# Four rounded-weight products, then four remainder products: the order of TensorE's matmuls within a unit of a split-precision decoder trunk

## What is computed

```python
def swiglu(h, w_gate, w_up, w_down):
    return (jax.nn.silu(h @ w_gate) * (h @ w_up)) @ w_down

for l in range(DEPTH):                                   # 2 layers
    x = x + 0.5 * swiglu(rmsnorm(x, norm_ffn1_g[l]), ffn1_w_gate[l], ffn1_w_up[l], ffn1_w_down[l])
    h = rmsnorm(x, norm_mix_g[l])
    proj = h @ w_in[l]                                   # 1024 x 5120
    ...
    merged = jax.nn.sigmoid(g_attn) * (attn @ w_branch_attn[l]) \
        + jax.nn.sigmoid(g_conv) * (conv @ w_branch_conv[l])
    x = x + merged @ w_out[l]
    x = x + 0.5 * swiglu(rmsnorm(x, norm_ffn2_g[l]), ffn2_w_gate[l], ffn2_w_up[l], ffn2_w_down[l])
return rmsnorm(x, final_g)
```

## Time and profile before

| | |
|---|---|
| median of 3 runs | 1111.26 us (1111.18 to 1115.11) |
| the profiled execution's own time | 1111.28 us |
| its span, from first to last instruction | 1109.5 us |
| TensorE matmuls | 6512, busy 1089.9 us (98%) |
| weight loads | 6512, busy 962.4 us (87%) |
| VectorE, ScalarE busy | 829.7 us (75%), 642.5 us (58%) |
| mean granted clock of TensorE | 0.995 of full speed |
| read from HBM | 199.32 MB, 181 GB/s over the span |

### The profile page before, as it was taken

One profiled execution on the slowest core, in us unless ns is written; L12 is line 12 of the kernel. 1 busy time (PEld: TensorE's weight loads), 2 busy tenths in 40 slices (PEclk: granted clock), 3 DMA queues, 4 the chain that ended last, 5 costly groups with the idle time before them and its releaser, 6 DMA issues.

```text
span 1109.5 us, 19933 instructions
## 1 busy us (share of the span) xinstructions
PE 1089.9 (98%) x6512; PEld 962.4 (87%) x6512; DVE 829.7 (75%) x1016; ACT 642.5 (58%) x908; POOL 19.9 (2%) x38
## 2 busy tenths in 40 slices
PE   7999999999999999999999999999999999999996
PEld 6888888888899988888888888888888998888885
DVE  5876767778898877776777776767788988677666
ACT  7655544556775655554465555445667656565454
POOL 6100000000000000000000000000000000000000
PEclk9999999999999999999999999999999999999998
DMA  8756555654566566656556656566455655656551
GB/s 221 243 180 199 175 169 188 208 172 152 175 188 188 170 193 187 190 178 191 191 167 186 206 172 198 162 208 194 147 157 184 195 175 184 202 173 205 173 190 39
DMA packets 202462, 201.76 MB, mean 182 GB/s; under 512 B 7904, under 2 KB 201472, under 8 KB 202416
## 3 DMA queue, kind: packets, MB, share of 16 engines
q1 hardware_dynamic: 200288, 199.25, 58.7%
q0 software_dynamic: 992, 1.87, 0.8%
q10 hardware_dynamic: 1136, 0.05, 0.1%
HBM read 199.32 MB, written 1.84 MB: 181 GB/s over the span
## 4 chain that ended last, share of the span: by engine, by line
PE 97%; ACT 1%; DMA 1%; DVE 1%; issue 0%; SPq 0%; DVEq 0%; ACTq 0%
PE acc L1114 57%; PE acc L1123 31%; PE acc L1118 4%; DMA raw<-in_ffn_w_gate_dram 1%; PE mixed L1118 1%; PE score L1118 1%; PE score L1224 0%; PE mixed L1156 0%; PE mixed L1123 0%; PE score L1123 0%; PE mixed L1245 0%; ACT w_hi L474 0%; PE mixed L1232 0%; PE mixed L1238 0%; ACT L508 0%
## 5 line engine op out<-in xcount | busy, mean ns | idle before, releaser
L1114 PE MATMUL acc<-xm,w_hi 128*128 128x512 f32 x2048 | 648.3, 398 | 4.3 <-ACT xt L565 2.4
L758 DVE TENSOR_TENSOR w_lo<-raw,w_hi 128x1024 fp32r<-128x1024 f32 (+1 forms) x387 | 455.7, 1200 | 141.9 <-ACT w_hi L474 141.2
L1123 PEld LDWEIGHTS acc<-xm,w_lo 128*128 128x128 f32 x2048 | 386.0, 188 | 91.5
L474 ACT CAST w_hi<-raw 128x1024 fp32r<-128x1024 f32 (+1 forms) x387 | 389.4, 1030 | 124.9 <-PE acc L1123 105.9
L1123 PE MATMUL acc<-xm,w_lo 128*128 128x256 f32 x2048 | 403.5, 278 | 0.0
L1114 PEld LDWEIGHTS acc<-xm,w_hi 128*128 128x128 f32 x2048 | 313.4, 189 | 5.2 <-issue 4.9
L1114 PE MATMUL acc<-hm,w_hi 128*128 128x512 f32 x704 | 221.1, 395 | 0.0
L1123 PEld LDWEIGHTS acc<-hm,w_lo 128*128 128x128 f32 x896 | 162.2, 189 | 31.3
L1123 PE MATMUL acc<-hm,w_lo 128*128 128x256 f32 x896 | 177.0, 279 | 0.0
L486 ACT COPY acc_lo<-acc 128x512 f32<-128x512 f32 x144 | 84.2, 585 | 130.3 <-PE acc L1123 130.1
L770 DVE TENSOR_TENSOR sum<-acc,acc_lo 128x512 f32<-128x512 f32 x144 | 99.2, 689 | 48.4 <-ACT acc_lo L486 48.1
(11 more groups left out here) (145 smaller groups left out, 463.8 us busy)
## 6 DMA issues: line engine op xcount, KB each, us to landing
raw<-in_ffn_w_gate_dram SPq DMA_DIRECT2D x88, 512.0 KB, 4.7
raw<-in_ffn_w_up_dram SPq DMA_DIRECT2D x88, 512.0 KB, 4.1
raw<-in_ffn_w_down_dram SPq DMA_DIRECT2D x80, 512.0 KB, 4.7
raw<-in_w_in_dram SPq DMA_DIRECT2D x80, 512.0 KB, 4.3
raw<-in_w_out_dram SPq DMA_DIRECT2D x16, 512.0 KB, 4.3
raw<-in_ffn_w_down_dram SPq DMA_DIRECT2D x16, 256.0 KB, 3.4
raw<-in_w_branch_attn_dram SPq DMA_DIRECT2D x8, 512.0 KB, 3.5
raw<-in_w_branch_conv_dram SPq DMA_DIRECT2D x8, 512.0 KB, 4.1
```

The lines of the kernel that those rows point to most:

```text
L474: nc.scalar.copy(w_hi[:, s, 0:tiles, :], raw[:, s, 0:tiles, :]).then_inc(hi_split, 1)
L758: nc.vector.tensor_tensor(w_lo[:, s, 0:tiles, :], raw[:, s, 0:tiles, :], w_hi[:, s, 0:tiles, :], ALU.subtract).then_inc(lo_split, 1)
L1114: nc.tensor.matmul(banks[:, m, :], w_hi[:, r, k, cols], x[:, 0:2 * SEQ], start=first and k == 0, stop=False, skip_group_check=True)
L1123: mm = nc.tensor.matmul(banks[:, m, 0:SEQ], w_lo[:, r, k, cols], x[:, 0:SEQ], start=False, stop=last and k == ends, skip_group_check=True)
```

## The change

Within a unit the K tiles are taken two at a time. For a pair of K tiles `multiply` issues the four hi products (two K tiles by two column tiles; eight matmuls with `halves=False`), and then the four lo products. Before, it was two (four) and two for each K tile. The matmuls themselves, their operands, the waits and the signal at the end are the same; the order in which the products are added changes.

```diff
-                for k, x in enumerate(x_tiles):
-                    for m in range(PAIR):
-                        cols = slice(m * P, (m + 1) * P)
-                        if halves:
-                            nc.tensor.matmul(banks[:, m, :], w_hi[:, r, k, cols], x[:, 0:2 * SEQ],
-                                             start=first and k == 0, stop=False, skip_group_check=True)
-                        else:
...
-                    for m in range(PAIR):
-                        cols = slice(m * P, (m + 1) * P)
-                        mm = nc.tensor.matmul(banks[:, m, 0:SEQ], w_lo[:, r, k, cols], x[:, 0:SEQ],
-                                              start=False, stop=last and k == ends, skip_group_check=True)
+                for k0 in range(0, len(x_tiles), 2):
+                    for k in (k0, k0 + 1):
+                        for m in range(PAIR):
+                            cols = slice(m * P, (m + 1) * P)
+                            if halves:
+                                nc.tensor.matmul(banks[:, m, :], w_hi[:, r, k, cols], x_tiles[k][:, 0:2 * SEQ],
+                                                 start=first and k == 0, stop=False, skip_group_check=True)
+                            else:
+                                for at_x in (0, SEQ):
+                                    nc.tensor.matmul(banks[:, m, 0:SEQ], w_hi[:, r, k, cols],
+                                                     x_tiles[k][:, at_x:at_x + SEQ],
+                                                     start=first and k == 0 and at_x == 0, stop=False,
+                                                     skip_group_check=True)
+                    for k in (k0, k0 + 1):
+                        for m in range(PAIR):
+                            cols = slice(m * P, (m + 1) * P)
+                            mm = nc.tensor.matmul(banks[:, m, 0:SEQ], w_lo[:, r, k, cols], x_tiles[k][:, 0:SEQ],
+                                                  start=False, stop=last and k == ends, skip_group_check=True)
                 mm.then_inc(used, 1)
```

## The result

The changed kernel takes 1117.99 us (median of 6 runs, 1117.15 to 1120.80), the kernel before 1111.22 us (6 runs). The ratio is 1.0058, 95% interval 1.0044 to 1.0071: slower by 0.6%, 6.8 us. That is inside the stated range (1104 to 1122), but just past what the prediction called no change (0.5%, 5.6 us); the interval reaches to both sides of that limit. The profiled execution took 1117.99 us, its span is 1116.2 us.

The account below looks back on a forecast made before the run. TensorE, busy 98% and hardly waiting, was taken as the bound: matmul count times start gaps. Terms -1 + 3 + 0 = +2 ns a pair, times 688 = +1.4 us, gave 1112.5 us; range 1104 to 1122.

Parts of the forecast that it names:

- no change: The whole kernel's time stays within 0.5%, 5.6 us or 8 ns a pair of K tiles; chance 70%.
- No added or removed work, no wait moved: In `multiply`, the same matmuls, weight loads, semaphore waits and slot release as before, so 0.
- `halves=False` at 0: In the 64 pairs with only 256-column matmuls, the steady run stays at 0.120 us a matmul, so 0.
- PSUM banks at 0: Two PSUM banks still alternate from one matmul to the next, so 0.
- a part of the lock that passes 5.6 us: Partial slowing of the lo gaps, or of the 512-column creep, costing more than 5.6 us; chance 7%.
- Crossings, -1 ns a pair: Hi/lo switches fall from four to two a pair of K tiles: -1 ns, bounds -6 and +4 ns.
- Longer runs of 256 columns, +3 ns a pair: Four lo matmuls in a row slow slightly: +3 ns a pair, bounds 0 and +20 ns.
- Longer runs of 512 columns, 0: Four hi matmuls in a row keep their gap: 0, upper bound +10 ns a pair, +6.9 us.
- lo start to hi start: Sign in the profile after: lo start to next hi start 0.46 to 0.465 if forecast, 0.48 if lo gaps lock.
- The short products lock: Rival: four lo gaps of each pair fall to 0.120 at once, +20 ns a pair, +13.8 us, 1125 us; 10%.
- The crossings cost: Rival: hi/lo switches cost 6 ns each, so two fewer save 12 ns a pair, -8.3 us, 1103 us; 13%.
- The reserve of loads: Within the 10% lock rival: long matmuls build a reserve of weight loads for two short ones, which four use up.

Follow-up runs that it names:

- twos: The order of the kernel before, two hi and two lo matmuls in turn, 256 columns for lo: 1111.22 us.
- alone: Hi and lo matmuls alternate one by one for each column tile, in place of the order of the kernel before: 1123.16 us, ratio 1.0109.
- 320 columns: Lo matmuls 320 columns wide instead of 256, against the kernel before: 1196.04 us in the old order (1.0763), 1189.96 in the new (1.0705).
- fours: The order of the changed kernel, four hi and four lo matmuls in turn, against the kernel before: 1117.99 us, ratio 1.0058.
- eights: All four K tiles of a unit at a time, eight hi then eight lo matmuls, against the kernel before: 1114.97 us, ratio 1.0026.
- 384-column pair: Lo matmuls 384 columns wide instead of 256, against the kernel before: 1288.95 us in the old order (1.1589), 1265.24 in the new (1.1373).

## Why the prediction held, and where it was off

**What bounds the kernel**: held. PE's waits (0.9 us more) and the clock are as before, and 688 times the longer pair are 6.5 of the 6.8 us.

**No added or removed work, no wait moved; `halves=False` at 0**: held, 0.120 a matmul there before and after. **PSUM banks at 0**: shown by the run with the crossings in one bank.

**"No change"**: just missed. The limit was 5.6 us or 8 ns a pair, and the medians are 6.8 us and the timeline 9.5 ns apart. What came is the case that was given 7%, a part of the lock that passes 5.6 us. The forecast itself was 1112.5.

**Crossings, -1 ns a pair**: the step that was wrong in kind. It read the start gaps of one pattern (hi to hi 0.232, hi to lo 0.235) and took them as prices that add up in another. The runs show that they don't: a hi gap is in the mean 0.2267 between equals, 0.2334 in twos, 0.230 in a run of eight, 0.2360 alone, and at 320 columns one sequence has two speeds. That inner gap and crossing were equal in the kernel before did not mean that crossings were free; both lay above the 0.2267.

**Longer runs of 256 columns, +3 ns a pair**: mis-sized. It measured +14 ns of the upper bound of +20. The entry row was taken for the nearest, but there the four short gaps come once, behind two hi; in the changed kernel they come after each four hi, at 0.1185.

**Longer runs of 512 columns, 0**: mis-sized. The hi side as a whole, this term and the crossings' together, came to -4 ns. It was the term named as the one that no row of before shows.

The sum was +2 ns a pair, measured +9.5. Of the signs named in advance, hi start to lo start came out as said (0.929 for 0.93), lo start to hi start between the two cases (0.474 for 0.46 or 0.48), the pair just past its limit (1.403 for 1.400). That the time lies in the range owes little to the sum. The range was set by the rivals, and its upper end left out only the full lock; and the lo term's miss of 11 ns was in part hidden by the 4 ns that the hi side gave back, which is luck. The likeliest case's own range (1107.5 to 1116) was too narrow by 2 us.

**Rivals.** The short products lock: its direction and part of it, 14 of 20 ns, came true; its point of decision, a mean lo gap over 0.117, was passed (0.1185). But the lo gap does not go by the length of its run alone (0.1174 alone, 0.115 in twos, 0.1185 in fours, 0.119 in eights), and as an account of the time the lock fails: eight and eight costs less than four and four. The crossings cost: not seen at 256 columns in this order; the 384-column pair shows that it would have been right there, 24 us faster with half of the crossings. The reserve of loads, which the prediction set beside the Trainium skill's statement that loads are pulled ahead of matmuls in flight (TensorE: Matmul & The Clock Gate, What happens when you issue a matmul), is excluded by the traces. In each of them the load of a matmul starts 2 ns or more after the start of the matmul ahead of it and never before it, in all 6245 cases where both are products with w_hi or w_lo. So loads are pulled ahead by one matmul, in every order, and no reserve builds up.

**What stays open.** Shown: only the sequences with unequal widths lie above the equal-width gap; by how much depends on the whole periodic sequence and, at 320 columns, on something that changed when other matmuls came between. That the starts fall into a fixed relation to something periodic in the engine or its memories, and keep it, is my reading of this; it was argued and not shown. What that something is was not found.

## What to carry to other kernels

Where TensorE is the bound and never waits, measure an order of matmuls of unequal width as a whole; don't add up gaps read from another order, since 256 beside 512 columns in twos (3.5 ns a K tile over the equal-width sum) and 384 beside 512 in twos (26.5 ns) behave quite differently. A steady run of equal widths gives the floor to compare with, and here no sequence went below it, so some 3.5 ns x 1376 = 4.8 us, 0.4%, is all that order could be expected to give (an estimate). Where a pattern repeats, don't average times that are rounded to 0.01 us: the rounding repeats with it. A bound on a term that no row shows is worth more than the value chosen inside it.

## What the runs showed of the hardware

- A steady run of fp32r matmuls of one width with a load each: a start every 0.2267 us at 512 columns, every 0.120 at 256.
- Loads of 128x128 fp32r weights come no closer than 0.108 us in any trace: lo matmuls of 128 columns in place of 256 save 14 of the 147 us that the columns alone would.
- The same instructions have two steady speeds: 0.7531 and 0.7669 a K tile at 320 beside 512 columns, at the same granted clock, with a change between them inside one stage.
- A load starts 2 ns or more after the matmul ahead of it, in 6245 of 6245 cases in each trace: it is ahead of its own matmul by one and no more.
- Two matmuls in a row into one PSUM bank cost nothing (0.9996, 0.9985 to 1.0007), and the switch of weights or moving tile costs nothing where all have 512 columns (1.2572 in both orders).
